# A value product in three float32r passes, and attention's loop written out

## The chip, the cores and the metric

The kernel runs on one core of a Trainium2 chip, in one launch. The core has TensorE (matrix products, weights loaded by a separate instruction), VectorE, ScalarE, GpSimd and SyncE, which only issues transfers here. The metric is the time of one execution on the device in microseconds (us). The result is float32 and must agree with the reference, so most products are made from two halves of each operand: a high half rounded to float32r, and a low half, the float32 remainder, also rounded. Three products, high x high, high x low and low x high, stand for one of full precision.

## The reference

One encoder layer over 2048 positions and 1024 features: a modulated norm, an input projection, latent attention beside a short gated convolution, an output projection, a mixture of experts and a final norm. The change touches attention only: 8 heads, queries and keys of 96 columns (64 plain, 32 rotated), values of 64, and a mask by chunks of 64 positions.

```python
q = (rms_norm(q_c, q_norm_g) @ w_uq).reshape(B, S, H, DN + DR)
kv = rms_norm(kv_c, kv_norm_g)
k_nope = (kv @ w_uk).reshape(B, S, H, DN)
v = (kv @ w_uv).reshape(B, S, H, DV)
...
s = (jnp.einsum('bqhd,bkhd->bhqk', qn, k_nope)
     + jnp.einsum('bqhr,bkr->bhqk', qr, k_rope)).astype(jnp.float32) * sm_scale
s = jnp.where(allowed[None, None], s, NEG_INF)
p = jax.nn.softmax(s, axis=-1).astype(v.dtype)
return jnp.einsum('bhqk,bkhd->bqhd', p, v)
```

## The kernel before, in words

The program runs its stages one behind another: `project`, `attend`, `mix`, `route`, `experts`, `combine`. In `attend` the scores are computed transposed, keys on the partitions and queries along the columns. Queries come in 4 groups of 512 (`GQ` = 4 tiles of 128). Group g meets the key tiles 0 to 4g+3, one step each (`STEP_OF`), so a head has 40 steps. In the last four steps of a group the chunk mask cuts off queries, and the step has 512, 384, 256 and 128 columns (`first_tile`). A head so has 28 steps of 512 columns and 4 each of the narrower ones.

A step m on TensorE is, in this order: the score of step m+1 (`score`, L874 to L876, three float32r products; the first carries the negated maximum and the mask as extra rows of its contraction), a plain score for the maxima of a tile that comes up 20 chunks later (`plain_scores`, L830), sometimes a part of the next head, and the value product of step m (`value`, L905). The value product is one float32 matmul; the profile records two instructions for it. Its stationary tile `VV` holds 64 columns of values and 64 ones, so the lower half of the output is the softmax's sum.

The other engines serve this order. ScalarE takes the exponential of a step's scores (L1123) and copies keys, queries, values, maxima and finished outputs. VectorE finds the maxima of the plain scores (L987, L990), rotates the queries (L972 to L975), makes the keys' low half (L966), and divides: two reciprocals (L998) and a multiplication (L1003). GpSimd makes the queries' low half (L1143) and the diagonal matrices from the maxima (L1149) that TensorE spreads over the rows (`spread_maxima`, L838).

While a head runs, the next one is prepared. `PART_AT` puts eight parts at steps 2, 5, 8 and so on: keys (L810, float32) and queries (L813, two float32 products) in turn. `V_AT` puts the values of the next two heads (L820) at four steps. `DIVIDE_AT` sets the steps at which VectorE divides a finished group. The order on each engine is that in which the code is written; engines meet only in counting semaphores. The loop runs over 4 pairs of heads. Behind the last head it prepares a head that doesn't exist, and its results are never read. The output of a group goes to DRAM (`mix_dram`), from where the next stage loads it.

## Time and profile before

| | |
|---|---|
| median of 3 runs | 2049.97 us (2049.68 to 2051.54) |
| the profiled execution | 2049.59 us, span 2047.8 us |
| TensorE busy in the span | 1854.8 us (91%) |
| VectorE, ScalarE, GpSimd busy | 1220.7 (60%), 728.3 (36%), 499.6 us (24%) |
| first and last value product start | 486.3 and 1103.2 us |

The profile is of one execution. Times count from the start of its span. A row of a timeline gives start, duration, engine, line of the kernel, operation, output and inputs, and shape; rows with "x2" merge neighbours. `tbank` is attention's PSUM tensor. PE is TensorE's matmul and PEld its weight load, DVE is VectorE, ACT ScalarE and POOL GpSimd. Durations of matmuls overlap their neighbours, so what one costs is read from the distance between starts.

### The profile page before, as it was taken

How to read it: one execution, taken by the hardware profiler on the slowest of the kernel's cores; microseconds unless marked ns; L12 is line 12 of the kernel's file. 1: busy time of each engine (PE TensorE's matmuls, PEld its weight loads, DVE VectorE, ACT ScalarE, POOL GpSimd, SP SyncE). 2: the span in 40 equal slices, each digit the busy share in tenths (PEclk: the TensorE clock that was granted, in tenths of full speed). 3: DMA queues.
4: the chain of work that ended last, by engine and by line, in shares of the span. 5: the costliest groups of instructions: out<-in, count | busy, mean ns of one | idle time of the engine just before them, and what ended most of it. 6: DMA issues, size and time to landing. Idle time of an engine off the chain costs nothing. (4 is left out here: it accounts for less than half of the span.)

```text
span 2047.8 us, 27274 instructions
## 1 busy us (share of the span) xinstructions
PE 1854.8 (91%) x8738; PEld 1438.2 (70%) x8738; DVE 1220.7 (60%) x2093; ACT 728.3 (36%) x1209; POOL 499.6 (24%) x550
## 2 busy tenths in 40 slices
PE   2899999997999999999996999983999999999970
PEld 2677878764666666666664788872899999999960
DVE  4688889856675675675674655546344444444434
ACT  3545353325444444444443332320222222222214
POOL 0131413112211211211221111103234343434330
PEclk8999999997999999999998899985999999999995
DMA  7655656410000000000002434414799999999948
GB/s 275 203 176 153 202 139 181 144 56 1 9 8 6 8 8 5 8 8 5 8 8 100 174 139 145 159 73 154 240 271 275 271 270 278 267 280 270 276 98 328
DMA packets 216160, 290.79 MB, mean 142 GB/s; under 512 B 24373, under 2 KB 172048, under 8 KB 215834
## 3 DMA queue, kind: packets, MB, share of 16 engines
q1 hardware_dynamic: 193498, 220.60, 32.5%
q0 software_dynamic: 20224, 69.22, 13.5%
q8 instruction: 28, 0.46, 0.1%
q10 hardware_dynamic: 2368, 0.17, 0.1%
q14 instruction: 42, 0.34, 0.1%
HBM read 229.13 MB, written 60.82 MB: 142 GB/s over the span
## 5 line engine op out<-in xcount | busy, mean ns | idle before, releaser
L905 PE MATMUL tbank<-probs,VV 128*128 128x512 f32 (+3 forms) x640 | 292.5, 538 | 1.3 <-ACT probs L1123 1.2
L987 DVE TENSOR_REDUCE cmax<-tbank 128x1 f32<-128x512 f32 (+2 forms) x340 | 206.0, 606 | 99.1 <-PE tbank L830 91.9
L1123 ACT ACTIVATE probs<-tbank 128x512 f32<-128x512 f32 (+1 forms) x320 | 169.7, 533 | 235.3 <-PE tbank L876 231.6
L387 PE MATMUL pbank<-hhi,wslhi 128*128 128x512 f32 x512 | 205.9, 402 | 8.2 <-DVE wsllo L440 6.8
L874 PE MATMUL tbank<-Qhi,Khi 97*128 97x512 f32 (+2 forms) x321 | 212.4, 662 | 0.0
L1881 DVE TENSOR_SCALAR xTe<-ebank,modcol 128x256 f32<-128x256 f32 (+1 forms) x128 | 53.8, 473 | 258.8 <-PE ebank L1799 137.5
L1149 POOL TENSOR_SCALAR diag<-cst,nmax 128x128 fp32r<-128x128 f32 x138 | 84.4, 612 | 486.1 <-DVE nmax L990 485.8
L387 PE MATMUL pbank<-hhi,wsllo 128*128 128x512 f32 x512 | 200.7, 392 | 0.0
L387 PE MATMUL pbank<-hlo,wslhi 128*128 128x512 f32 x512 | 200.6, 392 | 0.0
L1821 PE MATMUL ebank<-xTe,wg 128*128 128x192 f32 x1024 | 171.8, 326 | 3.1 <-DVE ahi L1909 1.8
L1821 PEld LDWEIGHTS ebank<-xTe,wg 128*128 128x128 f32 x1024 | 167.9, 190 | 7.9 <-DVE ahi L1909 2.1
L1821 PE MATMUL ebank<-xTe,wu 128*128 128x192 f32 x1024 | 171.6, 326 | 0.0
L1821 PEld LDWEIGHTS ebank<-xTe,wu 128*128 128x128 f32 x1024 | 167.3, 190 | 0.0
L905 PEld LDWEIGHTS tbank<-probs,VV 128*128 128x128 f32 x640 | 113.0, 190 | 60.0 <-issue 24.4
L2015 ACT ACTIVATE xTe<-ebank,modcol 128x256 f32<-128x256 f32 (+1 forms) x128 | 56.8, 509 | 233.8 <-PE ebank L1799 147.0
L830 PE MATMUL tbank<-Khi,Qhi 96*128 96x512 f32 (+2 forms) x340 | 128.5, 381 | 4.1 <-DVE cmax L987 3.4
L331 POOL DMA_DIRECT2D wmod<-in_w_ada x64 | 48.5, 757 | 304.8 <-DVE macc L519 294.9
L387 PEld LDWEIGHTS pbank<-hhi,wslhi 128*128 128x128 f32 x512 | 97.0, 189 | 31.9 <-DVE wsllo L440 8.2
L875 PE MATMUL tbank<-Qhi,Klo 96*128 96x512 f32 (+1 forms) x321 | 119.0, 371 | 0.0
L876 PE MATMUL tbank<-Qlo,Khi 96*128 96x512 f32 (+1 forms) x321 | 118.4, 369 | 0.0
L387 PEld LDWEIGHTS pbank<-hhi,wsllo 128*128 128x128 f32 x512 | 96.8, 189 | 21.0
L387 PEld LDWEIGHTS pbank<-hlo,wslhi 128*128 128x128 f32 x512 | 96.8, 189 | 20.6 <-issue 1.4
(273 smaller groups left out, 3491.4 us busy)
## 6 DMA issues: line engine op xcount, KB each, us to landing
wg<-in_w_exp_gate SPq DMA_DIRECT2D x32, 1024.0 KB, 6.3
wu<-in_w_exp_up SPq DMA_DIRECT2D x32, 1024.0 KB, 9.6
wd<-in_w_exp_down SPq DMA_DIRECT2D x32, 1024.0 KB, 7.4
wraw<-in_w_in SPq DMA_DIRECT2D x60, 512.0 KB, 4.1
wmod<-in_w_ada POOLq DMA_DIRECT2D x64, 256.0 KB, 3.4
xt<-in_x SPq DMA_DIRECT2D x4, 2048.0 KB, 11.0
wada<-in_w_ada SPq DMA_DIRECT2D x4, 2048.0 KB, 19.0
mixed<-mix_dram SPq DMA_DIRECT2D x16, 512.0 KB, 4.3
```

The lines of the kernel that those rows point to most:

```text
L387: ins = pe.matmul(out, w[:, S % 3, k], h[:, n % 2, k], start=k == 0 and j == 0, stop=k == KD - 1 and j == 2)
L830: pe.matmul(plain[:, chunk % 2, 0:w], Qhi[0:QKD, b, i * P:(i + 1) * P], Khi[0:QKD, b, n * 512:n * 512 + w], start=True, stop=True).then_in ...
L874: pe.matmul(out, Khi[0:every, b, k], Qhi[0:every, b, q], start=True, stop=False)
L875: pe.matmul(out, Klo[0:QKD, b, k], Qhi[0:QKD, b, q], start=False, stop=False)
L876: pe.matmul(out, Khi[0:QKD, b, k], Qlo[0:QKD, b, q], start=False, stop=True).then_inc(scores_done, 1)
L905: ins = pe.matmul(out, VV[:, kt, 2 * b:2 * b + 2].rearrange("p c d -> p (c d)"), step_of(probs, m), start=kt == 0, stop=last)
L987: W(ve.tensor_reduce(cmax[:, i % 2, n:n + 1], plain[:, chunk % 2, 0:w], AX.X, ALU.max), plain_read)
L1123: A(act.activation(step_of(probs, m), scores[:, m % 2, j * P:512], ACT.Exp), exp_done)
L1149: po.tensor_scalar(diag[:, i // GQ % 2, i % GQ * P:(i % GQ + 1) * P], cst[:, C_ID:C_ID + P], nmax[:, i:i + 1], None, ALU.mult).then_inc(di ...
L1821: ins = pe.matmul(out[:, f * CAP:(f + 1) * CAP], w[:, b, k, f * P:(f + 1) * P], xT[:, k, cols_of[b]], start=k == 0, stop=k == KD - 1)
L1881: return ve.tensor_scalar(xT[:, k, at], turn[:, 0, lo:lo + n], modc[:, 24 + k:25 + k], modc[:, 16 + k:17 + k], ALU.mult, ALU.add)
L2015: return act.activation(xT[:, k, at], turn[:, 1, lo:lo + n], ACT.Identity, scale=modc[:, 24 + k:25 + k], bias=modc[:, 16 + k:17 + k])
```

## The change

The values and the exponentials are split into halves (`VVhi`, `VVlo`, `phi`, `plo`) in float32r. The value product becomes `VVhi` x `phi`, `VVlo` x `phi` and, `LAG` = 2 steps later, `VVhi` x `plo` (`value_low`). ScalarE takes each exponential twice from the same scores, once rounded (`phi`) and once in float32 (`probs`, which now lies in the space of `KR`). GpSimd subtracts the two (`prob_low`) into a ring of 4 slots. VectorE makes the values' low half (`lower_values`). The ones beside `VVhi` meet zeros beside `VVlo`; ScalarE writes both ahead of the loop.

The division is parted: VectorE keeps the reciprocals (`invert`), GpSimd multiplies one step later (`divide`). The product of the rotation goes back into the PSUM bank of the product in place of an SBUF tile, and TensorE reuses this bank after the sum (`qf_ready`). A finished group is copied in two halves at steps 2 and 3 of the next group, where it was all at step 0. Parts behind the first come one step later, and the values two or three.

The loop over pairs is written out on all engines but SyncE, so that waits are against constants. With that `nothing_follows` leaves out, in the last head, the parts, values, maxima and scores of a head after it.

Excerpts of the diff:

```diff
-PART_AT = {2 + 3 * c: c for c in range(8)}
+PART_AT = {2 + 3 * c + (c > 0): c for c in range(8)}
...
-V_AT = [(1, STEPS_HEAD - NT + 4 * (v + 1)) if v < V_PARTS - 1 else (0, 1) for v in range(V_PARTS)]
+LAG = 2
+RING = 4
+V_AT = [(1, STEPS_HEAD - NT + 4 * (v + 1) + LAG) if v < V_PARTS - 1 else (0, LAG + 2) for v in range(V_PARTS)]
...
+def nothing_follows(hp, b):
+
+    return (hp, b) == (HEADS // 2 - 1, 1)
...
-            with pe.Fori(0, HEADS // 2) as hp:
...
+            def value_low(m, b, first):
+
+                g, kt = STEP_OF[m]
+                last = kt == GQ * (g + 1) - 1
+                pe.wait_ge(plo_done, first + (m + 1 + RING))
+                ins = pe.matmul(outp[:, g % 2, first_tile(g, kt) * P:512], heads_values(VVhi, kt, b),
+                                step_of(plo, m), start=False, stop=last)
+                if last:
+                    ins.then_inc(out_done, 1)
...
+            for hp in range(HEADS // 2):
                 for b in range(2):
                     head = hp * 2 + b
                     nxt = hp * 2 + (b + 1)
+                    end = nothing_follows(hp, b)
...
-                        ins = pe.matmul(out, VV[:, kt, 2 * b:2 * b + 2].rearrange("p c d -> p (c d)"),
-                                        step_of(probs, m), start=kt == 0, stop=last)
...
+                        pe.matmul(out, heads_values(VVhi, kt, b), step_of(phi, m), start=kt == 0, stop=False)
+                        pe.matmul(out, heads_values(VVlo, kt, b), step_of(phi, m), start=False, stop=False)
...
-                    W(ve.tensor_tensor(turned_q[NOPE:QKD], made[QKD:P], cs[QKD:P, at], ALU.mult), made_dve)
...
+                    W(ve.tensor_tensor(made[NOPE:QKD], made[QKD:P], cs[QKD:P, at], ALU.mult))
...
+            def lower_values(v, pair, src=made):
+                ve.wait_ge(v_copied, pair * V_PARTS + (v + 1))
+                at = slice(v * 4, (v + 1) * 4)
+                W(ve.tensor_tensor(VVlo[:, at, 0::2], src.rearrange("p (t c d) -> p t c d", c=2, d=VD),
+                                   VVhi[:, at, 0::2].bitcast(F32), ALU.subtract), v_lowered)
...
                 if r == 0:
                     ve.wait_ge(out_free, head * GROUPS + (g + 2))
...
-                    W(ve.tensor_tensor(on[:, p], raw[:, g % 2, 0], rs[:], ALU.mult), divided)
+                    ve.wait_ge(divided, head * GROUPS + (g + 3))
+                W(ve.reciprocal(rs[:, r * P:(r + 1) * P], raw[:, g % 2, 1, r * P:(r + 1) * P]),
+                  inverted if r else None)
...
-            W(ve.memset(outp[:, 1], 1.0), out_set)
...
+                v, k = (VVhi, VVlo)[n % 2], n // 2 * 2 + 1
+                A(act.activation(v[:, :, k], cst[:, C_ONE:C_ONE + VD].unsqueeze(1).to_broadcast([P, NT, VD]), ACT.Copy,
+                                 scale=1.0 - n % 2), filled)
...
-            act.wait_ge(out_set, 1)
+            act.wait_ge(rope_rest, 2)
...
+                        act.wait_ge(plo_done, hp * 2 * STEPS_HEAD + (b * STEPS_HEAD + m + 1))
+                        A(act.activation(step_of(phi, m), scores[:, m % 2, j * P:512], ACT.Exp), phi_done)
                         A(act.activation(step_of(probs, m), scores[:, m % 2, j * P:512], ACT.Exp), exp_done)
-                        if kt == 0:
-                            copy_out((g - 1) % GROUPS, hp * 2 + (b if g else b - 1))
+                        if kt in (LAG, LAG + 1):
+                            copy_out(kt - LAG, (g - 1) % GROUPS, hp * 2 + (b if g else b - 1))
...
+            def divide(g, head):
+
+                p = (g + 1) % 2
+                hold(po, stored[p], (head * 2 + (g + 1) // 2) * 32, passed_pool)
+                hold(po, inverted, head * GROUPS + (g + 2), passed_pool)
+                po.tensor_tensor(on[:, p], raw[:, g % 2, 0], rs[:], ALU.mult).then_inc(divided, 1)
+
+            def prob_low(m, count):
+
+                hold(po, exp_done, count, passed_pool)
+                po.tensor_tensor(step_of(plo, m), step_of(probs, m), step_of(phi, m).bitcast(F32), ALU.subtract
+                                 ).then_inc(plo_done, 1)
...
+                        prob_low(m, hp * 2 * STEPS_HEAD + (b * STEPS_HEAD + m + 1))
                         chunk, ahead = chunk_at(m)
```

The order of TensorE shows the change in a wide step. Before, at two neighbouring steps of a head:

```order
L874 MATMUL tbank<-Qhi,Khi 128x512
L875 MATMUL tbank<-Qhi,Klo 128x512
L876 MATMUL tbank<-Qlo,Khi 128x512
L829 REGISTER_ALU
L830 MATMUL tbank<-Khi,Qhi 128x512
L894 REGISTER_ALU
L905 MATMUL tbank<-probs,VV 128x512
```

The same place now; L882 to L884 are the score, L835 is the plain score:

```order
L882 MATMUL tbank<-Qhi,Khi 128x512 [waits exp_done]
L883 MATMUL tbank<-Qhi,Klo 128x512
L884 MATMUL tbank<-Qlo,Khi 128x512
L835 MATMUL tbank<-Khi,Qhi 128x512 [waits plain_read]
L925 MATMUL tbank<-phi,VVhi 128x512 [waits phi_done]
L926 MATMUL tbank<-phi,VVlo 128x512
L903 MATMUL tbank<-plo,VVhi 128x512 [waits plo_done]
```

One row has become three, the last of which belongs to the step two before; the register instructions of the loop are gone.

On GpSimd, before, in the second half of a head, where the first maxima of the next head fall due (`diag`) beside a low half of queries:

```order
L1149 TENSOR_SCALAR diag<-cst,nmax 128x128 [waits max_ready]
L135 ISA
L1149 TENSOR_SCALAR diag<-cst,nmax 128x128 [waits max_ready]
L135 REGISTER_ALU
L1143 TENSOR_TENSOR Qlo<-qf,Qhi 96x512 [waits qhi_done]
```

The same place now, steps 20 to 23 of the head:

```order
L1212 TENSOR_TENSOR plo<-KR,phi 128x512 [waits exp_done]
L1199 TENSOR_SCALAR diag<-cst,nmax 128x128 [waits max_ready]
L1212 TENSOR_TENSOR plo<-KR,phi 128x384 [waits exp_done]
L1199 TENSOR_SCALAR diag<-cst,nmax 128x128 [waits max_ready]
L1193 TENSOR_TENSOR Qlo<-qf,Qhi 96x512 [waits qhi_done]
L1207 TENSOR_TENSOR on<-raw,rs 128x256 [waits on_stored0,inverted]
L1212 TENSOR_TENSOR plo<-KR,phi 128x256 [waits exp_done]
L1199 TENSOR_SCALAR diag<-cst,nmax 128x128 [waits max_ready]
L1212 TENSOR_TENSOR plo<-KR,phi 128x128 [waits exp_done]
L1199 TENSOR_SCALAR diag<-cst,nmax 128x128 [waits max_ready]
```

Every low half of the exponentials stands in the same queue as the diagonals, which wait for VectorE, and as the division's multiplication.

On ScalarE, at the start of the loop, before:

```order
L1117 UNCONDITIONAL_BRANCH
L1117 ISA
L1123 ACT_TABLE_LOAD
L1123 ACTIVATE probs<-tbank 128x512
L1083 ISA
L1087 ACTIVATE raw<-tbank 64x256
L1088 ACTIVATE raw<-tbank 64x256
```

The same place now:

```order
L1170 ACT_TABLE_LOAD [waits plo_done,scores_done]
L1170 ACTIVATE phi<-tbank 128x512 [waits rope_rest]
L1171 ACTIVATE KR<-tbank 128x512
L1170 ACTIVATE phi<-tbank 128x384 [waits plo_done,scores_done]
L1171 ACTIVATE KR<-tbank 128x384
```

Each exponential stands there twice, the table is loaded once and no more in the loop, and the first exponential has a new wait (`rope_rest`) behind the table load.

## Rows read from the trace of the kernel before

**Rows 1.** The window of attention: length, PE, PEld, DVE, ACT, POOL busy (instructions), clock.

```profile
486.00:1104.00 618.00, 614.95 (x2268) 387.54 (x2268) 395.09 (x833) 283.28 (x565) 118.15 (x160) 1.00 0.03 7
```

**Rows 2.** The value product line: count, ns min/median/max, first and last start.

```profile
L905 PE MATMUL tbank<-probs,VV x640: 272/590/1217, 486.3 to 1103.3; 128*128 128x512 f32 x128, 128*128 128x256 f32 x32
```

**Rows 3.** Timeline of TensorE: start, us, engine, line, tiles, shape.

```profile
788.31 1.02 PE L905 MATMUL tbank<-probs,VV 128*128 128x512 f32 x2
...
792.15 0.81 PE L905 MATMUL tbank<-probs,VV 128*128 128x384 f32 x2
...
793.37 0.59 PE L905 MATMUL tbank<-probs,VV 128*128 128x256 f32 x2
...
794.04 0.40 PE L875 MATMUL tbank<-Qhi,Klo 96*128 96x512 f32 x1
...
794.75 0.39 PE L905 MATMUL tbank<-probs,VV 128*128 128x128 f32 x2
```

**Rows 4.** Timeline of the weight loads in the same stretch.

```profile
789.17 0.19 PEld L875 LDWEIGHTS tbank<-Qhi,Klo 96*128 96x128 f32 x1 [0.24 <-issue]
789.34 0.19 PEld L876 LDWEIGHTS tbank<-Qlo,Khi 96*128 96x128 f32 x1
...
791.67 0.19 PEld L875 LDWEIGHTS tbank<-Qhi,Klo 96*128 96x128 f32 x1 [0.24 <-issue]
791.80 0.19 PEld L876 LDWEIGHTS tbank<-Qlo,Khi 96*128 96x128 f32 x1
...
792.80 0.19 PEld L875 LDWEIGHTS tbank<-Qhi,Klo 96*128 96x128 f32 x1
792.91 0.19 PEld L876 LDWEIGHTS tbank<-Qlo,Khi 96*128 96x128 f32 x1
...
793.80 0.19 PEld L875 LDWEIGHTS tbank<-Qhi,Klo 96*128 96x128 f32 x1
...
794.98 0.19 PEld L875 LDWEIGHTS tbank<-Qhi,Klo 96*128 96x128 f32 x1
```

**Rows 5.** Timeline: a weight copy and the first keys product of a head.

```profile
719.85 0.18 DVE L958 COPY wk<-wuk 128x64 f32 x1
...
721.14 0.19 PEld L810 LDWEIGHTS tbank<-kvn,wk 128*64 128x64 f32 x2 [0.25 <-issue]
...
722.14 0.48 PE L905 MATMUL tbank<-probs,VV 128*128 128x256 f32 x1
```

**Rows 6.** Timeline of VectorE behind the loop's turn.

```profile
952.90 0.11 DVE L985 MEMSET tbank<- 64x64 f32 x1 [3.06 <-issue]
```

**Rows 7.** ScalarE: exponentials on the page (busy, mean ns), output copies by form.

```profile
L1123 ACT ACTIVATE probs<-tbank 128x512 f32<-128x512 f32 (+1 forms) x320 | 169.7, 533 | 235.3 <-PE tbank L876 231.6
...
L1088 ACT ACTIVATE raw<-tbank 64x256 f32<-64x256 f32 x65 | 24.7, 380 | 0.8
```

**Rows 8.** GpSimd by form: count, busy us, mean ns.

```profile
L1149 POOL TENSOR_SCALAR diag<-cst,nmax 128x128 fp32r<-128x128 f32 x128 | 78.4, 613 | 477.2 <-DVE nmax L990 477.2
L1143 POOL TENSOR_TENSOR Qlo<-qf,Qhi 96x512 fp32r<-96x512 f32 x32 | 40.7, 1272 | 24.4 <-ACT Qhi L1069 24.4
...
L1508 POOL TENSOR_TENSOR mlo<-mixed,mhi 128x1024 fp32r<-128x1024 f32 x16 | 38.4, 2399 | 205.1 <-ACT mhi L1468 205.1
```

**Rows 9.** Timeline: VectorE's multiplication beside GpSimd, and alone.

```profile
733.84 1.26 POOL L1143 TENSOR_TENSOR Qlo<-qf,Qhi 96x512 fp32r<-96x512 f32 x1
733.96 1.42 DVE L1003 TENSOR_TENSOR on<-raw,rs 128x256 f32<-128x256 f32 x1
...
746.01 0.42 DVE L1003 TENSOR_TENSOR on<-raw,rs 128x256 f32<-128x256 f32 x1
```

**Rows 10.** Timeline ahead of the loop: ScalarE's queries, VectorE's keys.

```profile
465.63 0.63 ACT L1069 ACTIVATE Qhi<-qf 96x512 fp32r<-96x512 f32 x1 [1.42 <-DVE qf L1025]
...
483.96 2.28 DVE L1007 TENSOR_TENSOR Klo<-KR,Khi 32x2048 fp32r<-32x2048 f32 x1
```

**Rows 11.** Waits of attention: who for whom, us in total, times, longest.

```profile
POOL diag L1149 <- DVE nmax L990: 477.2, 120, 8.7
```

More of the change, by code:

```diff
@@ L827, in plain_scores @@
                 w = key_cols(i, n)
-                if not (isinstance(seq, int) and seq < 2):
+                if seq >= 2:
                     pe.wait_ge(plain_read, seq - 1)
@@ L835, in spread_maxima @@
                 pe.wait_ge(diag_ready, head * NT + GQ * (g + 1))
-                if not (isinstance(head, int) and g == 0):
+                if head or g:
                     pe.wait_ge(neg_copied, head * GROUPS + g)
@@ L870, in score @@
                     pe.wait_ge(neg_copied, head * GROUPS + (g + 1))
-                if not (isinstance(head, int) and m < 2):
+                if head or m >= 2:
                     pe.wait_ge(exp_done, head * STEPS_HEAD + (m - 1))
@@ L912, in _ @@
                             score(m + LEAD, b, head)
-                        else:
+                        elif not end:
                             score(m + LEAD - STEPS_HEAD, 1 - b, nxt)
@@ L916, in _ @@
                         i, n = CHUNK_OF[chunk]
-                        if i % GQ == 0 and n == 0:
+                        if i % GQ == 0 and n == 0 and not (ahead and end):
                             pe.wait_ge(qlo_done, (nxt if ahead else head) * 4 + (i // GQ + 1))
-                        plain_scores(chunk, 1 - b if ahead else b, hp * 2 * STEPS_HEAD + (b * STEPS_HEAD + AHEAD + m))
-                        if m in PART_AT:
+                        if not (ahead and end):
+                            plain_scores(chunk, 1 - b if ahead else b, hp * 2 * STEPS_HEAD + (b * STEPS_HEAD + AHEAD + m))
+                        if m in PART_AT and not end:
                             c = PART_AT[m]
+                            if b == 0 and c == 1:
+                                pe.wait_ge(v_lowered, hp * V_PARTS + V_PARTS)
                             if c == 0:
@@ L1030, in _ @@
                         maximum(chunk, chunk)
-            W(ve.memset(outp[:, 1], 1.0), out_set)
             rope_low(1)
             W.wait()
-            with ve.Fori(0, HEADS // 2) as hp:
-                W.enter(hp, {dve_step: 2 * (3 + 4 + NT + GROUPS * 2), weights_ready: 2, made_dve: 16, qf_ready: 8,
-                             plain_read: 2 * STEPS_HEAD, max_ready: 2 * NT, divided: 2 * GROUPS})
+            for hp in range(HEADS // 2):
                 for b in range(2):
@@ L1079, in copy_maxima, with copy_out @@
                   neg_copied)
[L1081 to L1089 removed]
+            def copy_out(h, g, head):
+                if h == 0:
+                    act.wait_ge(out_done, head * GROUPS + (g + 2))
+                    act.wait_ge(divided, head * GROUPS + (g + 2))
+                half = slice(h * VD, (h + 1) * VD)
+                act.activation(raw[half, g % 2, 0], outp[0:VD, g % 2, h * 256:(h + 1) * 256], ACT.Copy)
+                ins = act.activation(raw[half, g % 2, 1], outp[VD:P, g % 2, h * 256:(h + 1) * 256], ACT.Copy)
+                if h == 1:
+                    A(ins, out_free)
             below = slice(QKD, QKD + 1 + GQ)
@@ L1115, in _ @@
                 mask_rows(1, n)
-            act.wait_ge(out_set, 1)
-            with act.Fori(0, HEADS // 2) as hp:
+            act.wait_ge(rope_rest, 2)
+            for hp in range(HEADS // 2):
                 for b in range(2):
@@ L1133, in _ @@
                             g, ahead = SPREAD_AT[m - 1]
-                            copy_maxima(g, 1 - b if ahead else b, hp * 2 + (b + ahead))
-            copy_out(GROUPS - 1, HEADS - 1)
+                            if not (ahead and end):
+                                copy_maxima(g, 1 - b if ahead else b, hp * 2 + (b + ahead))
+            for h in range(2):
+                copy_out(h, GROUPS - 1, HEADS - 1)
         @block.gpsimd
@@ L1160, in _ @@
                 diagonal(i, 0)
-            with po.Fori(0, HEADS // 2) as hp:
+            for hp in range(HEADS // 2):
                 for b in range(2):
                     for m in range(STEPS_HEAD):
+                        prob_low(m, hp * 2 * STEPS_HEAD + (b * STEPS_HEAD + m + 1))
                         chunk, ahead = chunk_at(m)
-                        if chunk in TILE_END:
+                        end = nothing_follows(hp, b)
+                        if chunk in TILE_END and not (ahead and end):
                             diagonal(TILE_END.index(chunk), hp * 2 + (b + ahead))
-                        if PART_AT.get(m - QUERIES_REST_AFTER, 0) % 2:
+                        if PART_AT.get(m - QUERIES_REST_AFTER, 0) % 2 and not end:
                             rest(PART_AT[m - QUERIES_REST_AFTER] // 2, 1 - b, hp * 2 + (b + 1))
+                        if m - 1 in DIVIDE_AT and DIVIDE_AT[m - 1][1]:
+                            d = DIVIDE_AT[m - 1][0]
+                            divide(d, hp * 2 + (b - 1 if d == GROUPS - 1 else b))
+            divide(GROUPS - 1, HEADS - 1)
 def mix(nc, T, st):
```

143 lines of the change are left out of this document (74 added, 69 removed).

## The prediction

> **What bounds the kernel now.** I began with the engines' shares of the span, where TensorE leads by far. The change touches only attention, so I took that stretch as one window next [rows 1]: in 618 us TensorE is busy for 615, VectorE for 395, ScalarE for 283, GpSimd for 118, and the granted clock is full (2.4 GHz). A busy TensorE need not be a limit, so I added up what it is asked to do. The 320 steps of the value product begin at 486.3 and end at 1103.2 [rows 2], 616.9 us or 77.1 a head.
>
> The recorded durations of matmuls overlap; the distance between starts is what they cost. Three starts of float32r products with 512 columns lie 0.71 apart (794.04 to 794.75 [rows 3]), 0.237 each. For narrow ones the weight loads show the pace: 0.175 with 384 columns, 0.125 with 256, 0.11 with 128 (789.17 to 789.34, 791.67 to 791.80, 792.80 to 792.91 [rows 4]). The value product is float32 and holds the array from its start to the second weight load of the next score, which can be issued only when the first score streams: 0.86 with 512 columns (788.31 to 789.17), 0.65 with 384 (792.15 to 792.80), 0.43 with 256 (793.37 to 793.80), 0.23 with 128 (794.75 to 794.98) [rows 3, 4].
>
> A head has 40 steps, 28 with 512 columns and four each with 384, 256 and 128. Four float32r products a step (three of the score, one plain score) are 4 x (28 x 0.237 + 4 x 0.41) = 33.1 us. The value product is 28 x 0.86 + 4 x 1.31 = 29.3. The next head's keys are four float32 products of 1.0 (721.14 to 722.14 [rows 5]) and its queries eight of 0.86: 10.9. Values are two groups of four 128-wide float32 products, 1.8, the spread of the maxima 4 x 0.237 = 1.0. Sum 76.1 of 77.1: TensorE is the bound, with 1 us of waits a head. I read the waits last. Part of them stands where the loop turns: VectorE idles for 3.06 us for no engine's sake [rows 6], and each turn has a table load of ScalarE.
>
> **The value product.** Float32 becomes three float32r products with the same columns. With 512 columns 3 x 0.237 = 0.71 takes the place of 0.86, 0.15 saved; with 384 it is 0.65 - 0.525, with 256 0.43 - 0.375, with 128 0.23 - 0.33, a loss. A head saves 28 x 0.15 + 4 x (0.125 + 0.055 - 0.10) = 4.5 us and asks for 71.5. Over 8 heads: 36 us. The new third weight load hides as the score's do, under a product of 0.237.
>
> **Nothing behind the last head.** Gone from its TensorE work: keys and queries 10.9, twenty plain scores (twelve with 512 columns, two with 384, three with 256, three with 128) 3.9, three groups of values 2.8, two spreads and a score 1.2. That is 18.8 of a head that would ask for 72.4 (it is the kind with three groups of values): 53.6 remain. ScalarE comes close to that with twice 21.2 of exponentials [rows 7] and some 7 of copies, GpSimd with 44 of low halves and 7 of diagonals and divisions (both below). So no more than these 18.8 is to be had.
>
> **What is added elsewhere.** ScalarE computes each exponential twice. Now it is busy 283.3 / 8 = 35.4 a head; with 169.7 / 8 = 21.2 more [rows 7] it has 56.6 of TensorE's 71.5. The bursts matter: where a group begins with narrow steps, steps 0 to 3 need about 6 us of ScalarE (exponentials 3.5, the outputs' four copies 1.5, keys 0.6 [rows 7, 10], gaps) while TensorE needs 5.7. A score bank is freed only when the second exponential is done. I take 0.5 us at steps 0 to 3, 0.5 at steps 20 to 23, and 0.5 where the maxima's row is copied behind the new exponentials.
>
> GpSimd's low half was never run with 128 rows and 512 columns. The nearest rows are 96 x 512 at 1.27 us and 128 x 1024 at 2.40 [rows 8]; their line gives 1.27, 0.99, 0.71 and 0.43 for 512, 384, 256 and 128 columns: 28 x 1.27 + 4 x 2.13 = 44.1 a head. With today's 118.2 / 8 = 14.8 and four divisions of 0.71 that is 61.7, 84% of the head's time. The score of step m is the first work of step m-1 on TensorE, its low product the last of step m+2. A wide step is 7 x 0.237 = 1.66, so 3 x 1.66 + 0.71 = 5.7 us lie between; both exponentials take 1.5 with their latency and the operation 1.27, which leaves 2.9 of slack. The tightest place is steps 20 to 23: lows 3.4, four diagonals 2.5, a rest of the queries 1.3, a division 0.7 are 7.9 us against 5.9 on TensorE; a backlog of 2 just fits. I take 0.2 us a head.
>
> VectorE loses four multiplications a head (0.42 us alone [rows 9]) and gains two subtractions over 512 columns, about 0.6 by Klo's 2.28 for 2048 [rows 10]; it stays far under TensorE. Its in-place rotation has the same three operations.
>
> Port contention is real here: beside GpSimd's operation of 1.26 us, VectorE's multiplication of two SBUF tiles took 1.42 [rows 9], and 0.42 when alone. That multiplication is what leaves VectorE. The addition of the rotation now reads one operand from PSUM. The four weight copies remain; they end 1.1 us before TensorE wants them (720.03 against 721.14 [rows 5]). Held for a whole low each they would be 4 x 1.27 late, 4 us beyond the slack; not held, 0. GpSimd is near the end of step 0's low when they start, so I take 0.3.
>
> The Trainium skill ("SBUF — State Buffer", section "SBUF: two separate sides") says that VectorE and GpSimd lock a shared port pair for a whole instruction, where VectorE uses its two-port mode or has two SBUF inputs. The row of 1.42 agrees. By that rule the copies, should they use that mode, would be held each time GpSimd is ahead, which is a rival below.
>
> **Loop written out.** The turn's waits go (1 of the waits per head is all there is). Waits of a head become 2: the 1.7 above plus 0.3 for the copies. The bounds are 0 (all hidden) and 5 (each of the four places a microsecond more). Reading straight code I cost at nothing: what hides it is that instructions are fetched ahead, as in the projection, which is written out and keeps TensorE as busy.
>
> **Before and behind the loop.** ScalarE gets seven fills. Three of those with 1024 columns (about 1.1 each, twice a 512-column exponential) stand ahead of the last queries' copy; its queue has 1.42 of slack there [rows 10], so the diagonals start some 1.8 later. The first exponential now waits for VectorE's Klo of the other buffer, which ended at 486.24 (483.96 + 2.28 [rows 10]), and the table load stands ahead of that wait, beside it. VectorE's memset of 512 columns goes, about 0.5 by the same rate. So the first value product comes at 486.24 + 1.8 - 0.5 + 0.6 + 0.1 for a semaphore, 488.2 in place of 486.3: about 2.0. Behind the loop two low products wait for the last exponential and GpSimd, and the last multiplication takes 0.71 for 0.42: 1.3. Together 3.3, between 1 and 7.
>
> **Sum.** Seven heads of 71.5 + 2 = 73.5 make 514.5, the last 53.6 + 2.2 = 55.8: 570.3 for 616.9, 46.6 less; with 3.3 back, 43.3 less. The profiled execution took 2049.6 (span 2047.8), the median is 2050.0, nearly the same: 2049.6 - 43.3 = 2006.3.
>
> **Rivals.**
> *All stalls hidden.* Then 16 us of waits go: 1990. For it: only 1 us of waits per head now. Against: ScalarE and GpSimd were at 46% and 19%, and now have bursts beyond TensorE's. Chance 0.15.
> *ScalarE or GpSimd sets the pace.* At 61.7 us of work, an in-order queue with diagonals that wait for VectorE can come to 77 a head, 7 x 3.5 = 25 more: 2031. Chance 0.15.
> *The copies of weights are held.* Seven times 4 us more, 28 less the 2 already taken: 2032. For it the 1.42 of rows 9; against it, a GpSimd operation that is mostly done when they start. Chance 0.06.
> *GpSimd's queue blocks: slower than before.* GpSimd waits for VectorE's maxima 120 times, 477 us, at most 8.7 [rows 11]. Today only diagonals stand behind such a wait; afterwards low halves do, that TensorE needs. If each of 16 diagonals a head costs one low half, 1.27, GpSimd needs 82 us a head: seven such and a last of 62 are 636, so 2049.6 + 19 + 3.3 = 2072. It decides from 43.3 / (7 x 16) = 0.39 us lost at each diagonal beyond the slack. Against: the maxima come about 1.4 us after the plain score, about when the next exponentials are done. Chance 0.07.
> *The three passes save nothing*, if float32r products with these weights go at another pace than the score's: 36 us back, 2042. Their shapes are the same, chance 0.02.
> The forecast has the rest, 0.55.
>
> **Numbers.** 2006.3, its own range 1994 to 2024. The range over the cases, 1990 to 2031, leaves out the slower case, the held copies and little else. A measurement of this kernel tells 0.2% (4 us) from no change. Faster has the forecast and all rivals but the blocked queue, some of them only partly: 0.91; same 0.02; slower 0.07.
>
> **What would show it.** The value product's three lines at starts 0.237 apart; heads 73 to 74 us long and a last one near 56; GpSimd lows near 1.27 and busy for about 62 a head; ScalarE about 57; the first value product near 488.2; no table load within the loop. Wrong would be: TensorE's loads waiting for the low half or for the second exponential more than 2 us a head, weight copies of a microsecond, or diagonals late at step 24.

## The result, and the profile after

The changed kernel takes 1999.41 us, the median of 4 runs (1998.83 to 2001.47), against 2049.97 before: a ratio of 0.9754 with a 95% interval of 0.9737 to 0.9771, 50.6 us less. The forecast was 2006.3, a gain of 43.3. The profiled execution has a span of 1996.9 us against 2047.8.

The window of attention, from the first value product to the last, in the columns of [rows 1]:

```profile
488.00:1052.00 564.00, 559.44 (x2515) 426.52 (x2515) 354.01 (x752) 404.07 (x866) 474.12 (x497) 1.00 0.03 8
```

It was 618 us long. TensorE is still busy for nearly all of it, and GpSimd for 474 of 564 in place of 118 of 618. The page's groups (busy us, mean ns, then idle time before and who ended it):

```profile
L1212 POOL TENSOR_TENSOR plo<-KR,phi 128x512 fp32r<-128x512 f32 (+1 forms) x320 | 352.3, 1118 | 44.8 <-ACT KR L1171 44.6
...
L1170 ACT ACTIVATE phi<-tbank 128x512 fp32r<-128x512 f32 (+1 forms) x320 | 170.7, 533 | 141.6 <-PE tbank L884 137.1
...
L1171 ACT ACTIVATE KR<-tbank 128x512 f32<-128x512 f32 (+1 forms) x320 | 169.2, 529 | 0.0
...
L925 PE MATMUL tbank<-phi,VVhi 128*128 128x512 f32 (+1 forms) x320 | 134.7, 421 | 3.8 <-ACT phi L1170 3.7
```

L1123's 169.7 us of exponentials [rows 7] now stand twice, as L1170 and L1171. By form the low halves and the rest of GpSimd's work are:

```profile
L1212 POOL TENSOR_TENSOR plo<-KR,phi 128x512 fp32r<-128x512 f32 x224 | 284.2, 1284 | 44.3 <-ACT KR L1171 44.1
L1199 POOL TENSOR_SCALAR diag<-cst,nmax 128x128 fp32r<-128x128 f32 x118 | 71.5, 606 | 48.7 <-DVE nmax L1023 47.2 <-ACT KR L1171 1.3
...
L1207 POOL TENSOR_TENSOR on<-raw,rs 128x256 f32<-128x256 f32 x32 | 23.5, 733 | 0.0
```

The diagonals' wait for VectorE has gone from 477 us [rows 11] to 47: that idle time was GpSimd's spare time, and the low halves fill it. One wide step on TensorE, score to score, in the columns of [rows 3]:

```profile
766.46 0.39 PE L882 MATMUL tbank<-Qhi,Khi 97*128 97x512 f32 x1
766.69 0.40 PE L883 MATMUL tbank<-Qhi,Klo 96*128 96x512 f32 x1
766.92 0.40 PE L884 MATMUL tbank<-Qlo,Khi 96*128 96x512 f32 x1
767.16 0.39 PE L835 MATMUL tbank<-Khi,Qhi 96*128 96x512 f32 x1
767.39 0.39 PE L925 MATMUL tbank<-phi,VVhi 128*128 128x512 f32 x1
767.62 0.39 PE L926 MATMUL tbank<-phi,VVlo 128*128 128x512 f32 x1
767.85 0.39 PE L903 MATMUL tbank<-plo,VVhi 128*128 128x512 f32 x1
768.07 0.40 PE L882 MATMUL tbank<-Qhi,Khi 97*128 97x512 f32 x1
```

Seven products in 1.61 us, 0.23 each. Below and in the expectations, the length of step m is the distance from the first pass of the score of step m, which TensorE issues one step ahead, to that of the score of step m+1. A step with 512 columns and nothing else in it is 1.61 to 1.64 us long. The same in the kernel before:

```profile
703.01 0.80 PE L874 MATMUL tbank<-Qhi,Khi 97*128 97x512 f32 x1
...
704.80 0.80 PE L874 MATMUL tbank<-Qhi,Khi 97*128 97x512 f32 x1
```

That is 1.79 us. A head is counted from the value product of its step 0 to that of the next head's. The first takes 73.7 us; then heads of 73.6 and 72.1 us follow in turn, 72.85 in the mean; from the last head's first value product to its last it is 52.7.

Three stretches say where the time went: the first value product starts at 488.0 (486.3 before), the last at 1051.5 (1103.3), and from the last one to TensorE's first work of the next stage it is 20.4 us (19.0). That is 1.7 - 53.5 + 1.4 = -50.4 of the span's -50.9.

### The profile page after: what moved, and what is told of

Read it like the earlier page. It is cut to its first block and busy times, and to the rows that moved or that the text cites. A ratio compares the mean times of both kernels' runs of the same rounds, so it can differ in the third digit from the quotient of the medians.

```text
span 1996.9 us, 26921 instructions
## 1 busy us (share of the span) xinstructions
PE 1804.3 (90%) x8987; PEld 1482.5 (74%) x8988; DVE 1181.1 (59%) x2015; ACT 854.9 (43%) x1520; POOL 855.0 (43%) x887
## 5 line engine op out<-in xcount | busy, mean ns | idle before, releaser
L1212 POOL TENSOR_TENSOR plo<-KR,phi 128x512 fp32r<-128x512 f32 (+1 forms) x320 | 352.3, 1118 | 44.8 <-ACT KR L1171 44.6
L1020 DVE TENSOR_REDUCE cmax<-tbank 128x1 f32<-128x512 f32 (+2 forms) x320 | 193.4, 605 | 106.4 <-PE tbank L835 101.2
L1170 ACT ACTIVATE phi<-tbank 128x512 fp32r<-128x512 f32 (+1 forms) x320 | 170.7, 533 | 141.6 <-PE tbank L884 137.1
L1171 ACT ACTIVATE KR<-tbank 128x512 f32<-128x512 f32 (+1 forms) x320 | 169.2, 529 | 0.0
L925 PE MATMUL tbank<-phi,VVhi 128*128 128x512 f32 (+1 forms) x320 | 134.7, 421 | 3.8 <-ACT phi L1170 3.7
L835 PE MATMUL tbank<-Khi,Qhi 96*128 96x512 f32 (+2 forms) x320 | 122.0, 384 | 5.4 <-DVE cmax L1020 5.1
L1573 POOL TENSOR_TENSOR mlo<-mixed,mhi 128x1024 fp32r<-128x1024 f32 x16 | 38.3, 2394 | 200.9 <-ACT mhi L1533 200.9
L903 PE MATMUL tbank<-plo,VVhi 128*128 128x512 f32 (+1 forms) x322 | 117.8, 366 | 0.3 <-POOL plo L1212 0.2
L884 PE MATMUL tbank<-Qlo,Khi 96*128 96x512 f32 (+1 forms) x320 | 117.9, 368 | 0.0
L926 PE MATMUL tbank<-phi,VVlo 128*128 128x512 f32 (+1 forms) x320 | 117.3, 367 | 0.0
```

The lines of the kernel that those rows point to most:

```text
L835: pe.matmul(plain[:, chunk % 2, 0:w], Qhi[0:QKD, b, i * P:(i + 1) * P], Khi[0:QKD, b, n * 512:n * 512 + w], start=True, stop=True).then_in ...
L884: pe.matmul(out, Khi[0:QKD, b, k], Qlo[0:QKD, b, q], start=False, stop=True).then_inc(scores_done, 1)
L903: ins = pe.matmul(outp[:, g % 2, first_tile(g, kt) * P:512], heads_values(VVhi, kt, b), step_of(plo, m), start=False, stop=last)
L925: pe.matmul(out, heads_values(VVhi, kt, b), step_of(phi, m), start=kt == 0, stop=False)
L926: pe.matmul(out, heads_values(VVlo, kt, b), step_of(phi, m), start=False, stop=False)
L1020: W(ve.tensor_reduce(cmax[:, i % 2, n:n + 1], plain[:, chunk % 2, 0:w], AX.X, ALU.max), plain_read)
```

## The experiments

The kernel before took 2051 to 2053 us on the chips of these runs, so kernels are compared by their ratio to it. A ratio of 0.001 is 2.05 us. The interval of one ratio is about 3 us to each side, that of a difference of two 4 to 5 us.

### The change in steps: loop, skip, passes

The loop written out in the kernel before, and nothing else:

```diff
-            with pe.Fori(0, HEADS // 2) as hp:
+            for hp in range(HEADS // 2):
```

> The kernel before with attention's loop over pairs written out and nothing else: float32 value product, a ninth head still prepared. In the trace of before, the three heads behind a turn of the loop lose about 1.8 us in steps 1 to 3 against the other heads, and the first head more. If the turn's waits are all that the loop costs: 5 to 6 us less, about 2044. If straight code costs fetches of its own: 2050 or more, with idle time without a releaser spread over the heads.

Measured: 2044.82, ratio 0.9974 (0.9964 to 0.9983): 5 us. In its trace the heads behind a turn of the loop take 75.4 us where they took 76.5 to 76.7, and the first value product starts at 484.2. Next, in that kernel, nothing prepared behind the last head, with the value product still float32:

```diff
+                        if not (ahead and end):
+                            plain_scores(chunk, ...)
```

> The kernel before, loop written out and nothing prepared behind the last head; the value product stays one float32 product. By the forecast's term the last head sheds 18.8 us of TensorE work: 19 below the run with the loop alone, about 2025. What is then left of the 50.6 us, some 25, would be the three passes net of what they cost on the other engines. If instead the last head is bound by ScalarE or VectorE, it would gain under 12 and stay above 2032.

Measured: 2027.39, ratio 0.9880 (0.9863 to 0.9897): 19.3 us more by the ratios and 17.4 by the medians, against 18.8 in the prediction. The complement is the changed kernel with the preparation kept:

```diff
 def nothing_follows(hp, b):
-    return (hp, b) == (HEADS // 2 - 1, 1)
+    return False
```

> The changed kernel, but the last head prepares a head behind it, as before. The sum of the forecast gives 18.8 us more, 2018. The step lengths of the changed kernel's trace give 73 us for a full head against 51.5 for the last one, 21.5 more, 2021: then the waits of a head (on ScalarE's exponentials) went with the preparation as well.

Measured: 2016.78, ratio 0.9833 (0.9817 to 0.9850), 16.2 us above the changed kernel's 0.9754. By the traces the skip shortens the last head from 76.7 to 58.2 us with the float32 product and from 72.0 to 52.7 with the passes, so its worth is about the same with either. The steps so far sum to 24.6 us; the passes with all that belongs to them must bring the other 25.8. In the heads between the first and the last that is 72.85 us in place of 76.5.

### The division's multiplication back on VectorE

The changed kernel with `on = raw * rs` issued by VectorE behind the second reciprocal, with the waits that it needs there:

```diff
+                    W(ve.tensor_tensor(on[:, p], raw[:, g % 2, 0], rs[:], ALU.mult), divided)
...
-                po.tensor_tensor(on[:, p], raw[:, g % 2, 0], rs[:], ALU.mult).then_inc(divided, 1)
```

> The changed kernel with the division's multiplication back on VectorE behind its reciprocals. Port contention: it was 0.42 us alone and 1.42 beside a GpSimd operation of 1.26; with GpSimd busy 84% of a head most of the 32 multiplications should take over 1 us, VectorE has 35% of its time free, and the total moves by 0 to +5 us. Rival: the multiplication on GpSimd is what delays the low halves; then taking it off GpSimd makes it faster by 3 us or more.

Measured: 2031.89, ratio 0.9909 (0.9892 to 0.9925). That is 32 us above the changed kernel, and 6 above the kernel with the loop written out, the skip and the float32 product. The expectation had 0 to 5. With this multiplication on VectorE the three passes gain nothing. The timeline of this kernel shows the place (start, us, engine; in brackets the idle time before and what ended it):

```profile
554.71 4.74 DVE L1043 TENSOR_TENSOR on<-raw,rs 128x256 f32<-128x256 f32 x1
554.83 0.61 POOL L1204 TENSOR_SCALAR diag<-cst,nmax 128x128 fp32r<-128x128 f32 x1
...
555.40 3.76 POOL L1210 TENSOR_TENSOR plo<-KR,phi 128x512 fp32r<-128x512 f32 x3
...
559.36 1.27 DVE L1020 TENSOR_REDUCE cmax<-tbank 128x1 f32<-128x512 f32 x2
...
560.10 0.19 PEld L835 LDWEIGHTS tbank<-Khi,Qhi 96*128 96x128 f32 x1 [3.16 <-DVE cmax L1020]
```

The multiplication takes 4.74 us where its shortest took 0.425. It ends 0.3 us behind GpSimd's row: the low half that was running when it started, a diagonal and three low halves without a pause (555.40 + 3.76 = 559.16). Behind it on VectorE stand the maxima, and TensorE may write a plain-score bank only when the maximum has been read: it stands for 3.16 us. [Rows 9] had shown 1.42 for 0.42 beside one GpSimd operation. The Trainium skill ("SBUF — State Buffer", section "SBUF: two separate sides") has the engine that comes second blocked for the whole of the other's instruction; the trace agrees on the lock, but here the block outlasts the instruction: VectorE got no turn between five of them.

That is not so everywhere. Of the 32 multiplications in the heads eight are held through a row (2.64 to 4.75 us). Nine others start beside a low half too, with GpSimd's next operation close behind it, and get their turn between the two:

```profile
511.35 0.70 DVE L1043 TENSOR_TENSOR on<-raw,rs 128x256 f32<-128x256 f32 x1
...
511.73 1.47 POOL L1198 TENSOR_TENSOR Qlo<-qf,Qhi 96x512 fp32r<-96x512 f32 x1
```

Here GpSimd's next operation is the longer one, 1.47 us where 1.28 is usual. What decides between the two cases isn't shown.

Against the second trace of the changed kernel (below) the seven heads are 2.4 to 4.7 us longer, 26 us in all. Part of it is TensorE's granted clock, the last but two of these columns:

```profile
560.50:563.50 3.00, 3.00 (x15) 2.51 (x15) 1.39 (x5) 1.22 (x3) 2.02 (x3) 1.00 0.19 49
...
712.50:715.50 3.00, 3.00 (x9) 2.32 (x8) 0.79 (x2) 1.08 (x2) 2.15 (x3) 0.50 0.09 22
```

In four of the seven heads it falls to 0.50 for 3.4 us behind the stall. These are 4.0 to 4.7 us longer, the others 2.4 to 3.3; between heads with the same order of work the difference is some 1.5 us, 6 in all. Another 4 us lie behind attention, and no run explains them.

### A second operand in SBUF

To see whether it is the two SBUF inputs that count, the rotation's product is written to an SBUF tile in place of PSUM, so that the addition behind it reads two SBUF tiles. Work and order are the same.

```diff
-                    W(ve.tensor_tensor(made[NOPE:QKD], made[QKD:P], cs[QKD:P, at], ALU.mult))
+                    W(ve.tensor_tensor(turned_q[NOPE:QKD], made[QKD:P], cs[QKD:P, at], ALU.mult))
```

> The changed kernel with the rotation's product again in an SBUF tile, so that VectorE's addition reads two SBUF tiles, four times a head. The run with the division on VectorE lost some 3 us a head in one place, where the multiplication took up to 4.75 us beside a row of GpSimd's low halves without idle time between. If VectorE waits for the whole row, the addition of step 24 or 25, behind GpSimd's backlog of steps 20 to 23, takes several us, and the time rises by 5 to 25 us. If it waits for one operation of 1.27 at most, the other free time covers it: within 3 us of the changed kernel.

Measured: 2007.93, ratio 0.9782 (0.9767 to 0.9797), 6 us above the changed kernel. The addition's row, in this kernel and in the changed one (count, ns min/median/max):

```profile
L1009 DVE TENSOR_TENSOR qf<-qf,turned_q x28: 682/683/2083, 506.9 to 982.7; 32x512 f32<-32x512 f32 x28
```

```profile
L1009 DVE TENSOR_TENSOR qf<-qf,tbank x28: 685/685/686, 504.1 to 975.6; 32x512 f32<-32x512 f32 x28
```

With an operand in PSUM it never takes longer than 0.686, though half of the 28 run beside a low half, and seven of them beside two in a row. With both in SBUF one of the four of a head takes 2.08, behind two low halves in a row, and that head's step 28 becomes 2.65 us in place of 1.99: 7 x 0.66 = 4.6 of the 6 us. The other three fall where GpSimd pauses. So for this addition the operand's place decides whether it can be held, and its hour whether it is.

### How much slack GpSimd has

Each diagonal is computed twice, 16 x 0.61 = 9.8 us more GpSimd work a head:

```diff
+                for ready in (twice, diag_ready):
+                    po.tensor_scalar(diag[...], cst[...], nmax[:, i:i + 1], None, ALU.mult).then_inc(ready, 1)
```

> The changed kernel with each of the diagonals computed twice on GpSimd, 16 x 0.61 = 9.8 us a head more, so 71 us of GpSimd work a head beside 73 us of time. This is the forecast's rival of a blocked queue, made true by a known amount. With the slack of 2.9 us at steps 20 to 23 used up: four diagonals more put the lows 2.5 us later there, most of it on TensorE, 7 x 2 to 7 x 4 us more, 2014 to 2028. If the queue has room everywhere: under 3 us more.

Measured: 2045.26, ratio 0.9966 (0.9957 to 0.9976), 43 us above the changed kernel. The waits of TensorE's loads in attention (total us, times, longest):

```profile
PEld tbank L903 <- POOL plo L1214: 33.2, 52, 2.0
```

In the changed kernel these loads wait for GpSimd for 0.7 us in all. GpSimd then has 60.7 + 9.8 = 70.5 us of work a head, and the heads behind the first take 78.4: it is late long before its load reaches the head's length, because the lows of a narrow and diagonal-rich stretch come in a burst (steps 24 to 27 take 10.2 us together in one kind of head and 11.7 in the other, where they took 7.8). The 9.8 us of work cost 5.5 us a head, where 2 to 4 were expected. In three heads the granted clock also falls to 0.50 for 3.4 us. The mechanism of the rival with the blocked queue is there, and its threshold is about borne out: it was to make the kernel slower than before from 0.39 us lost at each diagonal beyond the slack; of the 0.61 added 5.5 / 16 = 0.34 is lost, and the kernel is still 7 us faster than before.

### ScalarE's bursts

This kernel leaves out the second exponential; one element is copied in its place, so the low halves are of other data:

```diff
-                        A(act.activation(step_of(probs, m), scores[:, m % 2, j * P:512], ACT.Exp), exp_done)
+                        A(act.activation(probs[0:1, m % RING, 0:1], cst[0:1, C_ONE:C_ONE + 1], ACT.Copy), exp_done)
```

> The changed kernel without the second exponential: ScalarE writes one element in its place, so the low halves are of other data; everything else runs. ScalarE sheds some 13 us a head (what a small write costs stays). TensorE waits for the first exponential 32 us in the trace of the changed kernel. If ScalarE's bursts are what stalls it: 15 to 30 us less, 1970 to 1984. If TensorE's own work is the bound there too: under 6 us less.

Measured: 1995.14, ratio 0.9713 (0.9698 to 0.9728): in attention ScalarE is busy for 302 us in place of 404 (the small copy still takes 0.185 each time), and that brings 8 us. The expectation had under 6 or over 15. Steps 28 and 29 go from 1.99 and 1.90 to 1.67 and 1.62, 0.6 us a head or 4 of the 8; the other 4 are no more than two ratios can differ by. ScalarE's timeline in the changed kernel shows what crowds there:

```profile
755.01 0.59 ACT L1171 ACTIVATE KR<-tbank 128x512 f32<-128x512 f32 x1
755.49 0.37 ACT L1123 ACTIVATE raw<-tbank 64x256 f32<-64x256 f32 x1
755.87 0.38 ACT L1124 ACTIVATE raw<-tbank 64x256 f32<-64x256 f32 x1
756.15 0.62 ACT L1105 ACTIVATE Qhi<-qf 96x512 fp32r<-96x512 f32 x1
756.79 0.59 ACT L1114 ACTIVATE Qhi<-tbank 1x512 fp32r<-1x512 f32 x1
757.41 0.60 ACT L1170 ACTIVATE phi<-tbank 128x512 fp32r<-128x512 f32 x1
...
758.05 0.19 PEld L925 LDWEIGHTS tbank<-phi,VVhi 128*128 128x128 f32 x1 [0.53 <-ACT phi L1170]
```

Between the exponentials of two steps stand two output copies, the queries' copy and the maxima's row, 1.9 us in all.

### Spreading the output copies

So the output copies of one group move three and five steps later, to the steps 5 and 8 of the group behind it, and its division four:

```diff
+COPY_AT = [(2, 3), (2, 3), (2, 3), (5, 8)]
...
-DIVIDE_AT = {... (2, (30, 31)) ...}
+DIVIDE_AT = {... (2, (34, 35)) ...}
...
-                        if kt in (LAG, LAG + 1):
+                        if kt in COPY_AT[g]:
```

> A candidate that may beat the changed kernel: in a head's last group, the two halves of the copy of the group before are taken at that group's steps 5 and 8 in place of 2 and 3, and the division's steps 30 and 31 become 34 and 35. Now ScalarE has the copy, the queries and the maxima's row in steps 26 and 27, and TensorE's steps 28 and 29 are 2.00 and 1.89 long in place of 1.63. If these waits go and no others come: 0.6 us a head, 5 us in all, about 1994.5. If the waits only move to steps 30 to 33: no change.

Measured: 2006.97, ratio 0.9776 (0.9763 to 0.9789), 5 us above the changed kernel, where 5 below was hoped for. The aim was met: steps 28 and 29 are 1.51 and 1.61. But in the second, fourth and sixth head step 3 is 5.5 to 6.2 us long where it was 2.28. The timeline there:

```profile
711.31 0.16 DVE L1024 TENSOR_REDUCE nmax<-cmax 128x1 f32<-128x3 f32 x1
711.50 0.95 DVE L989 COPY wq<-wuq 128x192 f32<-128x192 f32 x1
...
712.16 0.68 POOL L1200 TENSOR_SCALAR diag<-cst,nmax 128x128 fp32r<-128x128 f32 x1
...
712.38 2.55 DVE L990 COPY wq<-wuq 128x32 f32<-128x32 f32 x1
...
712.81 2.08 POOL L1213 TENSOR_TENSOR plo<-KR,phi 128x384 fp32r<-128x384 f32 x3
...
715.17 1.97 PE L816 MATMUL tbank<-kvn,wk 128*64 128x512 f32 x2 [2.46 <-DVE wk L992]
```

The weight copies are held as the multiplication was: the second takes 2.55 us where 0.17 is usual, and ends with GpSimd's row of low halves. In the changed kernel the same four copies slip in before the low halves, beside the diagonal:

```profile
708.60 0.42 DVE L988 COPY wq<-wuq 128x192 f32<-128x192 f32 x1
708.88 0.65 POOL L1199 TENSOR_SCALAR diag<-cst,nmax 128x128 fp32r<-128x128 f32 x1
708.93 0.17 DVE L989 COPY wq<-wuq 128x32 f32<-128x32 f32 x1
...
709.50 2.11 POOL L1212 TENSOR_TENSOR plo<-KR,phi 128x384 fp32r<-128x384 f32 x3
```

The diagonal alone holds none of them there. One copy of the changed kernel is held: in the first head, the key weights' for 1.28 us in place of 0.18, in both traces.

The stall has a second price. TensorE's granted clock, in windows of that kernel before and behind the stall (the column behind GpSimd's busy time):

```profile
712.00:714.00 2.00, 0.70 (x6) 0.39 (x4) 2.00 (x2) 1.94 (x7) 2.00 (x4) 1.00 0.00 0
...
716.00:718.00 2.00, 2.00 (x5) 0.93 (x4) 0.31 (x1) 0.59 (x1) 0.00 (x0) 0.50 0.00 0
```

After standing idle for 2.46 us the engine goes on at 1.2 GHz in place of 2.4, and products with 512 columns start 0.43 us apart until 721.4. In the other two heads the clock is back after 3.4 us. So the step in which it stalled and the one behind it, together 3.62 us in the changed kernel, take 7.8 to 8.6.

### The weight copies taken out of the row's way

Is it the copies, or is GpSimd late because its division comes later? Only the key weights' copy stays at the head's start, the query weights' three come two steps later:

```diff
+                        if m == 2 and not end:
+                            W.wait()
+                            weights(1 - b, hp * 2 + (b + 1))
```

Four kernels ran on one chip, the last of them in the section after this one. The changed kernel again:

> The changed kernel once more, as the measure for the three beside it: 0.9754 of the kernel before, 2000 to 2003 us. A step 3 of 2.28 us and weight copies of 0.4 us at every head's start, as in its first trace.

Measured: 2001.02 (2000.69 to 2005.09), ratio 0.9763 (0.9748 to 0.9777). That is 2 us above its first ratio. Its trace has a first head of 75.7 us in place of 73.7, the next ones are as before. The kernel with later output copies and the weights apart:

> The kernel with the later output copies (2007 us), with the three copies of the query weights two steps later and only the key weights' copy at the head's start. In the kernel with the later output copies these copies took 0.95 and 2.63 us at the start of every second head, beside GpSimd's row of a diagonal and three low halves, and TensorE's step 3 took 5.5 to 6.2 us in place of 2.28. Theory A (the copies read and write SBUF alone and wait for GpSimd's whole row; TensorE waits for the key weights): that step goes back to about 2.3 us, the shorter steps 28 and 29 stay, and the time is 5 us below the changed kernel, 1994 to 1998. Theory B (the division four steps later puts GpSimd behind, whatever VectorE copies): step 3 stays over 5 us and the time at 2007.

Measured: 1997.54, but with a spread of 1992.0 to 2002.9 (the trace is of a run of 1993.0); ratio 0.9740 (0.9719 to 0.9760). Step 3 is 2.28 in every head but the first (2.40), steps 28 and 29 are 1.51 and 1.62. From the first value product to the last it is 557.0 us; it was 570.7 with the copies together. So it was the copies (theory A). The second head's start:

```profile
563.08 0.91 DVE L998 COPY wk<-wuk 128x64 f32<-128x64 f32 x1
...
563.74 0.63 POOL L1210 TENSOR_SCALAR diag<-cst,nmax 128x128 fp32r<-128x128 f32 x1
563.91 1.27 DVE L1027 TENSOR_REDUCE cmax<-tbank 128x1 f32<-128x512 f32 x2
564.35 2.10 POOL L1223 TENSOR_TENSOR plo<-KR,phi 128x384 fp32r<-128x384 f32 x3
565.22 1.35 DVE L992 COPY wq<-wuq 128x192 f32<-128x192 f32 x1
```

Both copies are still held, for 0.7 and 1.1 us, but of the first copy's 0.7 us only 0.24 reaches TensorE's load of the key weights, which comes 1.1 us after the copy's start, and the step is no longer for it. The query weights it wants four steps later. The milder move, output copies at the group's steps 4 and 6 and the division two steps later:

> The same move of the query weights, with the third group's output copies at the group's steps 4 and 6 and the division two steps later in place of four. Theory A: as the kernel with the weights apart, steps 28 and 29 together 0.5 to 0.8 us shorter than in the changed kernel, and the time 2 to 6 us below it, 1995 to 2000. Theory B: GpSimd is half as late, step 3 between 2.3 and 5.5 us, and the time above the changed kernel's.

Measured: 1997.31 (1995.98 to 1998.09), ratio 0.9737 (0.9723 to 0.9750). It is 3.7 us, 0.19%, under the changed kernel on the same chip, and their intervals touch. This is the fastest version with steady times, a gain just at what can be told. The trace has heads of 72.8 and 71.6 us in turn, 0.7 and 0.6 under the changed kernel's.

### What one pass is worth

The third pass is left out but for the last step of each group; GpSimd still computes every low half.

```diff
-                ins = pe.matmul(outp[...], heads_values(VVhi, kt, b), step_of(plo, m), start=False, stop=last)
                 if last:
+                    ins = pe.matmul(outp[...], heads_values(VVhi, kt, b), step_of(plo, m), start=False, stop=last)
```

> Leaves out the third pass of the value product but for the last of each group, 36 of 40 a head; GpSimd still computes every low half. By 0.232 us for 512 columns, 0.175, 0.125 and 0.11 for the narrow ones, TensorE is asked for 7.7 us less a head, 61 us over eight. Theory A (TensorE's columns set the pace): wide steps of 1.63 us become 1.40, the head 65 to 67 us, the time 1945 to 1955. Theory B (GpSimd at 60.7 us a head or ScalarE at 51 sets the pace by then): the head stays at 69 to 71 us and the time at 1975 to 1985.

Measured: 1978.77, ratio 0.9644 (0.9629 to 0.9659), 22 us under the changed kernel on the same chip (24 by the ratios). 36 products fewer a head should bring 61 if columns alone counted. Wide steps do become 1.39 (theory A), but neither theory foresaw the rest: in three heads the weight copies are held again (step 3 is 4.8 to 5.4), step 26 is 1.69 for 1.63, step 34 2.17 for 1.84, and TensorE's waits are now for GpSimd and the copies:

```profile
PEld tbank L882 <- POOL plo L1212: 17.7, 40, 1.0
...
PEld tbank L815 <- DVE wk L991: 7.3, 3, 2.4
```

Behind each of the three stalls the granted clock is 0.50, for 3.4, 6.8 and 10.2 us. But even the heads without held copies take 68.2 us, 3.9 less than 72.1 where the columns make it 7.7. The changed kernel is so near to GpSimd's and ScalarE's bursts that less work on TensorE is half lost.

## Why the prediction was right

*TensorE is the bound.* Right. It is busy for 559 of 564 us, leaving out ScalarE's second exponential brings only 8 us, and a pass less brings 22. But the margin is thin: by its columns that pass is worth 61.

*Pitch of the passes, 4.5 us saved a head.* About right. A wide step goes from 1.79 to 1.63, 0.16 less for the 0.15 forecast. But all float32r products start 0.23 apart and not 0.237, and narrow ones cost less than the 0.11 taken from the loads, where they stand right behind a wide one:

```profile
703.92 0.39 PE L903 MATMUL tbank<-plo,VVhi 128*128 128x512 f32 x1
704.15 0.22 PE L882 MATMUL tbank<-Qhi,Khi 101*128 101x128 f32 x1
704.21 0.27 PE L883 MATMUL tbank<-Qhi,Klo 96*128 96x128 f32 x1
704.32 0.28 PE L884 MATMUL tbank<-Qlo,Khi 96*128 96x128 f32 x1
```

By these distances (0.232, 0.176, 0.12 and some 0.09 us for 512, 384, 256 and 128 columns) a head asks for 7 x (28 x 0.232 + 4 x 0.386) + 13.7 = 70 us, an estimate; the forecast had 71.5.

*Waits of 2 us a head.* Somewhat low: by the same estimate 2.8. The copies' burst in steps 28 and 29 is 0.6 us of it, where the text had placed it at steps 0 to 3 and 20 to 23. That the two errors nearly cancel is luck: 72.85 us a head for 73.5. The first head, which starts at 1.2 GHz, took 73.7. Seven heads are 510.8 us for the forecast's 514.5.

*Nothing behind the last head, 18.8.* Right: 19.3 and 16.2 in the two experiments. The last head took 52.7 in place of 55.8: 53.6 was a demand of the same over-estimated products, and ScalarE (busy for 43.8 of the 52.7 us) and GpSimd (48.9) kept up. This is 3.1 us of the 6.9 by which the forecast was high; the seven heads are 3.7.

*Loop written out: the turn's waits go.* Right, 5 us by the experiment.

*Start +2.0 and tail +1.3.* Measured 1.7 and 1.4 in the first trace, 2.8 and 1.1 in the second. With the loop alone written out the start was at 484.2, with the skip as well at 485.1, one to two us earlier than before, which the text did not foresee. What is added ahead of the loop may so cost more than it said; no run separates it.

*GpSimd 61.7 us a head, low halves of 1.27, 0.99, 0.71 and 0.43.* Right: 60.7, and 1.28, 1.01, 0.73 and 0.46. ScalarE's 56.6 was too much: it is busy for 51.5, because neighbouring operations overlap (a row of 0.59 starts at 755.01, the next at 755.49).

*Port contention: "that multiplication is what leaves VectorE".* The fact was named and given no price. This was mis-sized most, though the forecast didn't rest on it: [rows 9] showed one held operation, 1 us, and I reckoned with single operations of GpSimd. A row of five can hold VectorE for 4.7 us, and the move is worth 32 us, some 6 of them by the clock. Without it the result would have been 2032.

*Weight copies, +0.3.* Right in both traces of this kernel but for one held copy in the first head, and by luck of place. I gave the rival 0.06 and priced it at 4 us a head; the kernel with later output copies shows it in three of seven heads, at 4 to 5 us each, after a shift of a few tenths. Its mechanism is the row and the clock, not a wait for a low at each copy.

*The blocked queue.* It did not come. With 9.8 us more work a head it does, and costs 43 us.

*Range.* 1999.4 lies within 1994 to 2024. It lies on the side of the case with all stalls hidden (1990), but it was not that case: the waits stayed, and TensorE's work was less than reckoned.

The cause is settled for the loop, the skip and the division's place. Three things stay open: how much of the passes' 26 us lies in the pitch and how much in what came with them (the parts and divisions one or two steps later, the output copies in halves, the rotation in PSUM), as no run had these beside the float32 product; what lets VectorE in between two operations of GpSimd at one time and not at another; and why the weights-apart kernel's times spread over 11 us, in part with the granted clock (0.954 in the fastest run, 0.944 in the slowest).

## What to carry to other kernels

Where GpSimd works in long rows, look on VectorE for every operation that reads two SBUF tiles or copies SBUF to SBUF, and allow for the length of GpSimd's whole row as the upper bound, with the queue behind it; give it an operand in PSUM, move it to the engine that holds the port, or put it where the row pauses and nobody waits. When such a copy is harmless, ask how many tenths of a microsecond it has to spare before another step is shifted. When a small shift makes a kernel slower, compare the same step over all heads: one head in two tells more than a mean.

## What the runs showed that I had not expected

- VectorE's operation often does not get in between GpSimd's back-to-back operations: 4.74 us beside a diagonal and four low halves, 2.08 beside two low halves, where 0.425 and 0.683 are the undisturbed times. Nine multiplications of 32 did get in, and GpSimd's next operation then took 0.19 us longer.
- Behind an idle stretch of TensorE of 1.8 to 2.7 us its granted clock could go from 2.4 to 1.2 GHz: in three heads of three in the kernel with later output copies (for 3.4, 6.8 and 3.4 us), in four of seven in the one with the multiplication on VectorE (3.4 each). An idle stretch of 2.7 left it at 2.4 in one head, and one of 1.8 did not in another.
- Attention starts at 1.2 GHz, in the first trace of the changed kernel until 491.5 and in the second until 496.8. The first head is 73.7 and 75.7 us long there, about 2 us between two executions of one kernel.
- A float32r product with 128 columns costs 0.06 us right behind a wide one and 0.11 behind another narrow one.
